# Experts' output products one step later, in two parts, each beside products of its own tile width

## What is computed

```python
def hierarchical_moe(x, w_group, b_group, w_router, b_router, w_gate, w_up, w_down):
    ...  # top-1 group, then top-2 experts in it; combine: 512 x 16 weights
    hid = jax.nn.silu(jnp.einsum('td,edf->etf', t, w_gate)) * jnp.einsum('td,edf->etf', t, w_up)
    hid = hid * combine.T.astype(hid.dtype)[:, :, None]
    y = jnp.einsum('etf,efd->td', hid, w_down)
```

## Time and profile before

| | us |
|---|---|
| median of the runs | 1433.3 |
| span of the profiled execution | 1422.4 |
| TensorE busy | 1349.7 |
| VectorE busy | 582.7 |
| ScalarE busy | 350.6 |
| GpSimd busy | 400.9 |
| one step of the expert loop | 17.3 |

### The profile page before, as it was taken

The page is one execution under the profiler, slowest core; times in us unless marked ns, Lnnn a source line. Parts: engine busy times, 40 slices in busy tenths (PEclk is TensorE's granted clock), DMA queues, the critical chain, the costliest instruction groups (busy, mean ns, idle before and its releaser), DMA issues. The chain is left out here.

```text
span 1422.4 us, 24576 instructions
## 1 busy us (share of the span) xinstructions
PE 1349.7 (95%) x10332; PEld 813.1 (57%) x10332; DVE 582.7 (41%) x1401; ACT 350.6 (25%) x828; POOL 400.9 (28%) x458
## 2 busy tenths in 40 slices
PE   6989998899999997999999989999999999999997
PEld 5876545567888645444444435457777445655543
DVE  4355324572231534421211133554369581433415
ACT  3216225452101010101111123454211301322221
POOL 7650402206362651122222131020241002111062
PEclk9999999999999997999999999999999999999999
DMA  8290013400313347999999981011040421300131
GB/s 270 112 366 5 2 60 90 180 2 5 118 59 118 135 147 284 331 379 353 382 381 382 389 323 74 22 61 46 17 175 30 120 89 39 128 3 17 60 120 59
DMA packets 99792, 210.97 MB, mean 148 GB/s; under 512 B 14613, under 2 KB 22640, under 8 KB 99552
## 3 DMA queue, kind: packets, MB, share of 16 engines
q1 hardware_dynamic: 87152, 171.39, 33.6%
q0 software_dynamic: 12528, 37.97, 7.8%
HBM read 188.88 MB, written 19.42 MB: 146 GB/s over the span
## 5 line engine op out<-in xcount | busy, mean ns | idle before, releaser
L1560 POOL TENSOR_TENSOR AR<-Wt,AR 128x512 f32<-128x512 f32 x68 | 88.6, 1324 | 128.4 <-PE pb L1757 94.3
L3886 PE MATMUL pb<-Wt,HT 128*128 128x512 f32 x256 | 117.8, 602 | 1.1 <-DVE AR L3977 1.1
L1560 POOL TENSOR_TENSOR AR<-Wt 128x512 f32<-128x512 f32 x34 | 44.2, 1319 | 170.3 <-DMA Wt<-in_w_in_dram 80.3
L800 ACT ACTIVATE AR<-AR,SM 128x512 f32<-128x512 f32 (+3 forms) x128 | 70.9, 554 | 66.6 <-DVE SM L758 65.8
L2444 PE MATMUL pb<-AR 128*64 128x512 f32 x256 | 85.0, 595 | 0.7 <-issue 0.7
L758 DVE CUSTOM_DVE_ANT_0 AR<-pb,AR 128x512 f32<-128x512 f32 (+3 forms) x128 | 58.3, 488 | 63.0 <-PE pb L712 62.4
L1757 PE MATMUL pb<-AR 128*128 128x256 f32 x320 | 73.2, 380 | 3.7 <-issue 1.8
L3886 PEld LDWEIGHTS pb<-Wt,HT 128*128 128x128 f32 x256 | 46.3, 190 | 52.9 <-issue 49.3
L2444 PE MATMUL pb<-Wt,AR 128*64 128x512 f32 x192 | 70.8, 595 | 0.0
L712 PE MATMUL pb<-AR 64*128 64x512 f32 (+7 forms) x256 | 62.4, 492 | 8.0 <-DVE SM L758 5.2
L2651 POOL DMA_DIRECT2D ys<-AR x28 | 15.0, 542 | 189.9 <-ACT AR L2615 189.9
(11 more groups left out here) (581 smaller groups left out, 2530.8 us busy)
## 6 DMA issues: line engine op xcount, KB each, us to landing
Wt<-in_w_in_dram SPq DMA_DIRECT2D x18, 2048.0 KB, 8.5
AR<-in_w_gate_dram SPq DMA_DIRECT2D x8, 2048.0 KB, 18.0
AR<-in_w_up_dram SPq DMA_DIRECT2D x8, 2048.0 KB, 18.6
AR<-in_w_down_dram SPq DMA_DIRECT2D x8, 2048.0 KB, 17.7
Wt<-in_w_gate_dram SPq DMA_DIRECT2D x6, 2048.0 KB, 18.1
Wt<-in_w_down_dram SPq DMA_DIRECT2D x6, 2048.0 KB, 14.3
Wt<-in_w_up_dram SPq DMA_DIRECT2D x6, 2048.0 KB, 20.6
ys<-AR POOLq DMA_DIRECT2D x2, 3072.0 KB, 25.7
```

Source lines behind the costliest of these rows:

```text
L800: st.activation(s, s, ACT.Exp, bias=self.nm[i][:, h:h + 1], scale=-1.0, accum_out=self.rs[i][:, h:h + 1]).then_inc(s_pr, 1)
L1560: r = gt.tensor_tensor(out[:, k:k + s, :], a[:, k:k + s, :], b[:, k:k + s, :], op)
L3886: r = mm(s, HT[:, k, t * 128:(t + 1) * 128], W.ap(("gate2", c, br))[:, k, :], start=k == 0, stop=k == 7)
```

## The change

The output products of expert b move from step b+2 to step b+3 and are cut in two: `down_first` (the `ya` part) follows `first_rows`, `down_last` (the `yb` part) follows `last_rows`. A function `downs_at` says which experts' output products a step has: experts 12 and 13 are both done in step 15 (as before in 14 and 15), 14 in 16 and 15 in 17, as before. ScalarE's and VectorE's copies follow. The order of the weight loads is changed alike: `ed` of an expert is loaded behind `eg` and `eu` of the expert two further on (one further on before). GpSimd keeps its order, except that the stores of experts 12 and 13 come in one step, and a wait for `yb` 12 before the final gathers is dropped.

```diff
+        downs_at = lambda step: {14: (12, 13), 15: (14,), 16: (15,)}.get(step, (step - 2,) if step > 1 else ())
         for step in range(17):
             if step < 16:
                 W.plan(("eg", step), 8, 512, 1, ering)
                 W.plan(("eu", step), 8, 512, 1, ering)
-            if step > 0:
-                W.plan(("ed", step - 1), 4, 1024, 1, ering)
+            for b in downs_at(step):
+                W.plan(("ed", b), 4, 1024, 1, ering)
...
-            def down(b):
+            def down_first(b):
                 pe.wait_ge(*P.drained(("ht", b)))
                 pe.wait_ge(*W.loaded(("ed", b)))
...
                 r.then_inc(P.full(("ya", b)), 1)
+
+            def down_last(b):
+                w = W.ap(("ed", b))
                 s = P.take(pe, "O", ("yb", b))
...
             for step in range(18):
-                for stage, b in ((first_rows, step - 1), (turn, step), (hidden_turn, step - 2), (last_rows, step - 1),
-                                 (down, step - 2)):
...
+                downs = downs_at(step - 1)
+                if 1 <= step <= 16:
+                    first_rows(step - 1)
+                if step < 16:
+                    for b in downs[0:1]:
+                        down_first(b)
+                if 1 <= step < 16:
+                    turn(step)
+                if 2 <= step:
+                    hidden_turn(step - 2)
...
+                if 1 <= step <= 16:
+                    last_rows(step - 1)
+                if step < 16:
+                    for b in downs[0:1]:
+                        down_last(b)
+                for b in downs[1:] if step < 16 else downs:
+                    down_first(b)
+                    down_last(b)
...
-                for stage, b in ((first_rows, step - 1), (turn, step), (last_rows, step - 1), (down, step - 2)):
+                for stage, b in ((first_rows, step - 1), (turn, step), (last_rows, step - 1),
+                                 *((down, b) for b in downs_at(step - 1))):
...
-                for stage, b in ((first_rows, step - 1), (hidden_turn, step - 2), (last_rows, step - 1),
-                                 (down, step - 2)):
+                downs = downs_at(step - 1)
+                early = downs[0:1] if step < 16 else ()
+                for stage, b in ((first_rows, step - 1), *((down, b) for b in early), (hidden_turn, step - 2),
+                                 (last_rows, step - 1), *((down, b) for b in downs[len(early):])):
...
-            pipe(blocks, fetch, None, None, lambda b: store(b) if b < LATE else None)
+            for step in range(17):
+                if step < 16:
+                    fetch(step)
+                for b in downs_at(step - 1):
+                    if b < LATE:
+                        store(b)
...
             po.wait_ge(*P.filled(("gb", 14)))
-            po.wait_ge(*P.filled(("yb", 12)))
...
             ahead = [(n, name, b) for step in range(17)
-                     for n, name, b in (("eg", "w_gate", step), ("eu", "w_up", step), ("ed", "w_down", step - 1))
-                     if 0 <= b < 16]
+                     for n, name, b in (("eg", "w_gate", step), ("eu", "w_up", step),
+                                        *(("ed", "w_down", b) for b in downs_at(step))) if b < 16]
```

More of the change, by code:

```diff
@@ L2485, in moe_pe @@
             for step in range(18):
-                for stage, b in ((first_rows, step - 1), (turn, step), (hidden_turn, step - 2), (last_rows, step - 1),
-                                 (down, step - 2)):
[L2488 to L2495, removed]
+                downs = downs_at(step - 1)
[8 more added lines that the diff above has]
+                    hidden_turn(step - 2)
+                if step == 4:
+                    places_pe()
+                if step == 6:
+                    over_count(pe)
+                if step == 9:
+                    late_turn_pe()
+                if 1 <= step <= 16:
[6 more added lines that the diff above has]
+                    down_last(b)
         g2 = [[AR[:, 4096 + 1024 * (2 * t + j):5120 + 1024 * (2 * t + j)] for j in range(2)] for t in ALLT]
```

## The result

The changed kernel takes 1437.1 us (median of 20 runs, 1433.5 to 1440.8) against 1433.2 us (20 runs, 1428.0 to 1437.9): ratio 1.0029, 95% interval 1.0018 to 1.0041. The loss is small, 4 us, and under the 0.5% that the prediction took as the least that can be told, but it is clear of zero, and two later comparisons gave 1.0029 (1.0009 to 1.0050) and 1.0038 (1.0023 to 1.0053).

The account below looks back on a forecast made before the run. TensorE's own queue was taken as the bound, busy 95% of the span. Terms -4.3 + 4.8 + 1.5 - 2.3 - 1.7 + 1.7 = -0.3 us gave a median of 1433 us, range 1427 to 1444.

Parts of the forecast that it names:

- part 3: Token gather, issued at T+3.12 (T: step start) of its own step, lands late for `turn` at T+10.44; 4.8 us lost.
- Part 1: TensorE's column-split changes per step fall from five to three; 26 x 0.165 = 4.3 us gained, bounds 0 and 4.3.
- rival B: `turn` in steps 4 to 15: late gathers stall TensorE, with clock falls; slower, 1445; chance 0.2.
- Part 4: Step 3: TensorE waits before `hidden_turn(1)` for VectorE, busy with routing arithmetic; 1.5 us lost.
- Part 5: Waits for VectorE behind `turn` at steps 4, 9 and 5 vanish or shrink; 2.3 us gained.
- Part 6: TensorE's clock: the fall at step 5 goes (1.7 us gained), one at step 3 comes (1.7 lost); they cancel.
- Part 7: Reordered weight loads and the kernel's end: no weights late while part 3 holds TensorE back; 0 us.
- The base: Profiled span 1422.4 against median 1433.3: the 10.9 us difference, part of it outside the span, carried over unchanged.
- Rival C: Adjacent TensorE phases of the same split still pay 0.165, so the 4.3 us are missing; 1437; within the forecast's 0.6.
- Rival A: The gather lands by T+10.44, in time for `turn`; -5.1 us, 1428; chance 0.2, with rival D.
- rival D: Weights late at steps 15 and 16, only if rival A holds; takes back 1 to 3 us; chance 0.2 together with A.

Follow-up runs that it names:

- after_again: The changed kernel run again unaltered, for a second profile; ratio to the kernel before 1.0029.
- fetch_places: fetch_early with VectorE's routing arithmetic of step 2 put behind its 32-row product of that step; 1424.3 us, ratio to the kernel before 0.9920.
- unsplit_free: The changed kernel with output products whole behind the 32-row products, a step later than before, and the next gather issued ahead of each store; 1438.0 us, ratio 1.0061.
- fetch_early: The changed kernel with the gather of expert b+4 issued between the `ya` and `yb` stores of expert b; 1422.4 us, ratio to the kernel before 0.9907.
- fetch_first: The changed kernel with the gather behind the same wait for the `yb` copy but ahead of the four `yb` stores; ratio to the kernel before 0.9957.
- unsplit: fetch_early with output products whole behind the 32-row products, the gather still hanging on the `ya` copy; ratio to the kernel before 1.0253.
- fetch_gb15: fetch_early with the eight final gathers held until expert 15's 32-row products are done, instead of expert 14's; ratio to the kernel before 0.9982.
- before_free: The kernel before with only GpSimd's order changed, the next expert's gather issued ahead of each store; ratio 0.9996.

## Why the prediction was wrong, step by step

The forecast was 1433, a change of -0.3 us, which is to say none; the measured is +4. The place of nearly every effect was right; the size of part 3 was not, and the sum of six small terms of both signs stood on it.

- **Part 1, mode changes, nearly right.** Taken 0.165 each and nothing for neighbours of the same split; measured 0.14 (17.31 - 17.02 for two). The rows of the step above show why: 64-row products to `ya` 6.91 us and not 6.84, 32-row products to `yb` 3.48 and not 3.42. A boundary within the same split still costs 0.06 to 0.07 here. 26 x 0.14 = 3.6 us in place of 4.3. Rows 5, two groups of 128x128 tiles, did not carry over to this boundary.
- **Part 3, the gather: the step that failed.** The mechanism and its place were right (issue at T+3.12, TensorE ready near T+10.45, a wait of TensorE for the gather in 11 or 12 of the twelve steps, 10 forecast). The size was 4.8 us; the three profiles show 6.4, 9.7 and 6.4. The landing times of before were carried over one by one. The medians of the changed kernel's are only 0.1 to 0.2 higher (7.7, 7.8, 7.7 for 7.6), but the shortest are 7.4, 7.6 and 7.3 where before had 7.0: hardly a gather was in time, and each tenth counts twelve times. In after_again the second and third of the twelve take 9.1 and 9.4 us, where before had 7.1 and 8.0: this is beyond the half microsecond that the prediction named as a sign of being wrong. The line of after_again:

```profile
DMA to landing us min/median/max: 7.6/7.8/9.4
```

  A step that waits is also some 0.06 us longer than its wait (17.97 - 0.89 = 17.08 against 17.02), 0.7 us over eleven such steps, a term that the prediction did not have. And the falls of the clock behind such waits, put only into rival B, belonged into the forecast: in one profile of three they cost 6.8 us more. Loops of 262.9, 272.7 and 262.8 us are on average 4.4 us above before's, near the measured 3.9. That nearness proves little: the two short ones are of the fourth fastest of 20 runs and the fastest of ten, the long one of the slowest of twelve. The two short loops are only 1.1 to 1.2 us above before's, and that most of the rest of the 4 us is falls of the clock in the other runs is argued, not shown.
- **Part 4, step 3, right:** 1.5 us forecast, 1.4 to 1.5 found in every profile with the split products but fetch_places.
- **Part 5, right:** the waits for VectorE at steps 4 and 9 are gone, that of step 5 is 1.0 us (forecast 0.85): 2.1 us in place of 2.3.
- **Part 6, half right:** the fall at step 5 is gone. The fall at step 3 did not come in any changed profile, 1.7 us better than forecast. The yardstick, the length of one idle piece, was poor: 1.45 us at step 3 did not bring a fall, 1.01 us at step 4 of after_again was followed by one of 6.8 us, and at step 5 1.69 us brought one in the kernel before, 1.70 us in unsplit_free none.
- **Part 7, right** in that nothing was displaced: the weights are late only when the gathers are not, and then by 0.2 to 1.6 us.
- **The base.** Of the 10.9 us between the first profile's span of 1422.4 and the median, 6.9 are that profile's short piece behind step 16; the prediction left open what they are and put part of them outside the span. This did no harm, since both kernels pay that piece.

For the first profile the measured terms give -3.6 + 6.4 + 0.7 + 1.5 - 2.1 - 1.7 = +1.2, and the loop shows +1.2.

Of the rivals, B (the gather takes TensorE over) was the direction in which it went, with a third of its price (4 in place of 12 us). Rival C was put at 1437, just what was measured, but by luck: its mechanism, the full 0.165 between neighbours of the same split, is refuted by the 6.91 and 3.48 us above. Rival A, the gather in time, was put at 1428; the experiments that made it true gave 1422 to 1426. In the loop fetch_early gained 5.1 and 5.3 us in its two profiles, the predicted 5.1, and that is partly luck: the smaller gain of part 1 (3.6 for 4.3) and 0.8 us of waiting for weights (rival D) were made up by the fall at step 5 that did not come (1.7). The rest of its gain is 3 us behind step 16 and some us that single profiles don't show.

## What to carry to other kernels

When work is moved a step later, follow every loop that is paced by it: here GpSimd's loop had not been touched, yet its prefetch slid a whole step, because it stood in program order behind a store of the moved result. A prefetch whose arrival comes to lie within a microsecond of its use costs more than the mean says, since it is paid on the late side only and a stalled TensorE may lose its clock as well. The best version is the change with the gather issued ahead of the wait: 1422.4 and 1423.3 us, 0.7 to 0.9% faster than before.

## What the runs showed of the hardware

- While the weights stream (DMA share 1.00 to 1.05), an indirect gather of 96 rows of 4 KB lands 7.0 to 9.4 us after issue, whether it stands behind four stores or ahead of them (median 7.7 in fetch_first too). One that went out at 598.64 in fetch_early, where the share over the next 4.4 us was 0.55, landed in 4.3 us.
- The length of one idle piece of TensorE did not tell whether the clock fell behind it to the 1.2 GHz level. It did behind 1.01 us (after_again) and 1.69 us (before), and it did not behind 1.45 us (the changed kernel), 1.70 us (unsplit_free) and 2.97 us (unsplit, at 839.52). A fall in the loop cost 1.7 us in most cases and 3.4 us in one.
- During the first 11.4 to 11.7 us of the eight final gathers TensorE's completions were reported 5 to 8 us late in all profiles but the first of before (in fetch_gb15 later ones than the bank of expert 15, so that they moved with the gathers), and products were issued with gaps of 0.3 to 0.8 us. What holds TensorE there, and whether it is as long without the profiler, stays open; so does why the piece behind step 16 is shorter in the split kernels with early gathers (29.7 to 30.7 against 33.1 to 34.3), for before_free and unsplit_free have early gathers too and 33.1 and 33.2 us.
